# A deeper attention pipeline with a shorter second score pass, in a streaming encoder kernel

## The reference, cut to what matters

```python
def band_attend(q, kb, vb, bias, key_valid):
    s = jnp.einsum('bnthd,bnmhd->bnhtm', q, kb).astype(jnp.float32) * (HEAD_DIM ** -0.5)
    s = s + bias.astype(jnp.float32)[None, None]
    s = jnp.where(key_valid[None, :, None, None, :], s, NEG_INF)
    p = jax.nn.softmax(s, axis=-1).astype(vb.dtype)
    return jnp.einsum('bnhtm,bnmhd->bnthd', p, vb)
```

## Time and profile before

| | |
|---|---|
| Time, median of 3 runs | 2631.17 us (2630.45 to 2631.81) |
| Time of the profiled execution | 2631.02 us |
| Its span in the profile | 2629.2 us, so 1.8 us lie around it |
| PE busy | 2567.8 us, 98% of the span |
| DVE, ACT, POOL busy | 1771.9, 1356.9, 556.9 us |
| Attention stage, from its first score product to the first merge product | 775.1 to 1013.15 us, 238 us |

### The profile page before, as it was taken

One profiled execution on the slowest core, in us unless ns is written; L12 is line 12 of the kernel. 1 busy time (PEld: TensorE's weight loads), 2 busy tenths in 40 slices (PEclk: granted clock), 3 DMA queues, 4 the chain that ended last, 5 costly groups with the idle time before them and its releaser, 6 DMA issues.

```text
span 2629.2 us, 49866 instructions
## 1 busy us (share of the span) xinstructions
PE 2567.8 (98%) x18164; PEld 1678.0 (64%) x18164; DVE 1771.9 (67%) x3413; ACT 1356.9 (52%) x2632; POOL 556.9 (21%) x645
## 2 busy tenths in 40 slices
PE   6999899999999999999999999999999999999998
PEld 2466566666666665559986666666666666666665
DVE  5967577587746665566787798888888874242433
ACT  4967374564747773124566555555555553121211
POOL 2600000000017772000001354434333321101000
PEclk8999999999999999999999999999999999999999
DMA  8622513233365432555542445554555449566662
GB/s 294 201 87 88 197 52 137 93 124 133 104 181 122 114 121 107 181 191 148 146 117 86 142 171 176 185 182 157 174 185 180 138 136 349 196 246 233 236 247 95
DMA packets 243890, 424.07 MB, mean 161 GB/s; under 512 B 58424, under 2 KB 163384, under 8 KB 235528
## 3 DMA queue, kind: packets, MB, share of 16 engines
q1 hardware_dynamic: 234872, 413.08, 47.6%
q10 hardware_dynamic: 8848, 8.74, 1.0%
HBM read 284.47 MB, written 139.92 MB: 161 GB/s over the span
## 4 chain that ended last, share of the span: by engine, by line
PE 83%; DVE 5%; ACT 4%; DMA 3%; issue 2%; POOL 2%; SPq 1%; DVEq 0%; ACTq 0%; POOLq 0%
PE ps L3064 55%; PE ps L3319 14%; PE ps L3173 7%; PE ps L3163 2%; PE ps L3145 2%; PE ps L3132 1%; PE ps L3105 1%; POOL arena L1194 1%; ACT arena L1653 1%; DMA arena<-in_w_down 1%; DVE arena L2734 1%; ACT arena L1363 1%; DMA arena<-in_w_mod 1%; ACT arena L1329 1%; DMA arena<-in_w_mod_rest 1%
## 5 line engine op out<-in xcount | busy, mean ns | idle before, releaser
L3064 PE MATMUL ps<-arena 128*128 128x352 f16 (+1 forms) x11880 | 1612.8, 297 | 4.1 <-ACT arena L1821 1.9
L3064 PEld LDWEIGHTS ps<-arena 128*128 128x128 f16 x11880 | 1100.6, 97 | 511.8 <-ACT arena L1821 2.6
L3319 PE MATMUL ps<-arena 128*128 128x352 f16 x2772 | 415.0, 310 | 1.5 <-DVE arena L2763 1.2
L3319 PEld LDWEIGHTS ps<-arena 128*128 128x128 f16 x2772 | 264.7, 96 | 151.8 <-DVE arena L2763 1.5
L1226 POOL TENSOR_TENSOR arena<-arena 128x640 f32<-128x640 f32 (+5 forms) x136 | 150.2, 1123 | 707.5 <-DVE arena L2514 706.1
L1245 POOL TENSOR_TENSOR arena<-arena 128x128 f32<-128x128 f32 x44 | 30.9, 703 | 747.2 <-DMA arena<-in_w_down 746.9
L3173 PE MATMUL ps<-arena 128*128 128x424 f16 (+1 forms) x960 | 171.5, 341 | 0.0
L1813 ACT ACTIVATE arena<-ps 128x352 f32<-128x352 f32 x264 | 116.0, 460 | 94.7 <-PE ps L3064 94.7
L2866 DVE TENSOR_TENSOR arena<-ps,arena 128x352 f32<-128x352 f32 x12 | 6.3, 525 | 204.5 <-PE ps L3319 174.6
L3173 PEld LDWEIGHTS ps<-arena 128*128 128x128 f16 x960 | 92.5, 96 | 78.6
L1446 ACT ACTIVATE arena<-ps 128x352 f32<-128x352 f32 x192 | 80.4, 460 | 118.9 <-PE ps L3064 118.9
(11 more groups left out here) (239 smaller groups left out, 3293.4 us busy)
## 6 DMA issues: line engine op xcount, KB each, us to landing
hidden_combinations<-arena SPq DMA_DIRECT2D x48, 616.0 KB, 3.2
arena<-hidden_combinations SPq DMA_DIRECT2D x24, 1232.0 KB, 7.5
arena<-in_w_up SPq DMA_DIRECT2D x44, 512.0 KB, 5.0
down_combinations<-arena SPq DMA_DIRECT2D x44, 448.0 KB, 2.8
ffn_hidden<-arena SPq DMA_DIRECT2D x44, 440.0 KB, 3.1
arena<-down_combinations SPq DMA_DIRECT2D x10, 1792.0 KB, 7.6
arena<-down_combinations SPq DMA_DIRECT2D x20, 896.0 KB, 6.3
arena<-ffn_hidden SPq DMA_DIRECT2D x50, 352.0 KB, 4.0
```

What stands on the lines that cost most here:

```text
L3064: mm = pe.matmul(out, wt[:, k, wp, :], act_t[:, k, hp], start=(first and k == 0 and n == 0), stop=(last and k == K - 1 and n == 2), skip_g ...
L3319: mm = pe.matmul(ps[:, down_bank(n, k), 0:CF].rearrange("p (w t) -> p w t", w=2), dwt(i)[:, wi, wp, :], dact[i][:, :, bi, hp, :], start=(i ...
```

## The change

It has four parts.

1. Order on PE: scores of tile c, then the transposes of tile c - 2, then the value products, which come one cycle later than before (`Group.end` is one more). DVE and ACT get new orders to match, and one cycle more at the end. `inverse_sums` of head 1 moves into the next cycle.
2. Three probability buffers in place of two; the waits that guard them are loosened (`t_filled` by two units).
3. The second score pass contracts only the high half of the queries (64 rows) with the low part of the keys. Head 0 lies on partitions 0 to 63 and head 1 on 64 to 127. The order of the score products is new too: the first pass of both heads, then the short second pass of both heads in alternation. `s_filled` of both heads is raised at the end.
4. The low keys are stored once, not twice: per head group two loads fewer (10 in place of 12 on `at_loaded`), half the bytes of low keys, and two steps of `cached_halves` fewer (6 in place of 8).

```diff
-        pr = [at_(o, 2 * BAND).rearrange("p (h n) -> p h n", h=2) for o in (45120, 13056)]
+        pr = [at_(o, 2 * BAND).rearrange("p (h n) -> p h n", h=2) for o in (45120, 13056, 14336)]
...
-                self.end = self.last.tile + (3 if self.m < LOTS - 2 else 2)
+                self.end = self.last.tile + (4 if self.m < LOTS - 2 else 3)
... (ACT)
-            for c in range(NTILE + 2):
-                if c < NTILE:
-                    exps(Unit(2 * c))
-                for G in ended_in(c):
+            for c in range(NTILE + 4):
+                for G in ended_in(c - 1):
                     out_hi(G)
-                if c < NTILE:
-                    exps(Unit(2 * c + 1))
-                if 0 < c <= NTILE:
-                    for h in range(2):
-                        probs(Unit(2 * c - 2 + h))
+                for h in range(2):
+                    if 2 <= c < NTILE + 2:
+                        probs(Unit(2 * c - 4 + h))
+                    if c < NTILE:
+                        exps(Unit(2 * c + h))
... (DVE)
-            for c in range(NTILE + 2):
+            for c in range(NTILE + 4):
                 if c < NTILE:
                     scores(Unit(2 * c))
-                    scores(Unit(2 * c + 1))
-                    inverse_sums(Unit(2 * c))
                 if 0 < c <= NTILE:
-                    probs(Unit(2 * c - 2))
-                for G in ended_in(c):
+                    inverse_sums(Unit(2 * c - 1))
+                for G in ended_in(c - 1):
                     out_lo(G)
                 if c < NTILE:
-                    inverse_sums(Unit(2 * c + 1))
-                if 0 < c <= NTILE:
-                    probs(Unit(2 * c - 1))
+                    scores(Unit(2 * c + 1))
+                if 2 <= c < NTILE + 2:
+                    probs(Unit(2 * c - 4))
+                    probs(Unit(2 * c - 3))
+                if c < NTILE:
+                    inverse_sums(Unit(2 * c))
... (PE)
+                pieces = [(bank, c, x.k0 + 512 * bank) for bank, c in ((0, min(x.w, 512)), (1, x.w - 512)) if c > 0]
+                q = slice(x.q0, x.q0 + x.rows)
+                for y in units:
+                    keep_above_zero(pe, s_added, y.u - 1)
+                    for bank, c, k in pieces:
+                        pe.matmul(ps[0:x.rows, 2 * y.h + bank, 0:c], qs[x.b][:, y.h, q], khh[x.b][:, y.h, k:k + c],
+                                  start=True, stop=False)
+                for bank, c, k in pieces:
+                    for y in units:
+                        hi = slice(64 * y.h, 64 * y.h + 64)
+                        mm = pe.matmul(ps[0:x.rows, 2 * y.h + bank, 0:c], qs[x.b][hi, y.h, q], kll[x.b][hi, k:k + c],
+                                       start=False, stop=True)
...
-            for c in range(NTILE + 2):
+            for c in range(NTILE + 3):
                 if c < NTILE:
-                    scores(Unit(2 * c))
-                    scores(Unit(2 * c + 1))
+                    scores(Unit(2 * c), Unit(2 * c + 1))
+                if 2 <= c < NTILE + 2:
+                    probs(Unit(2 * c - 4))
+                    probs(Unit(2 * c - 3))
                 for G in parts_in(c):
                     outs(G, c)
-                if 0 < c <= NTILE:
-                    probs(Unit(2 * c - 2))
-                    probs(Unit(2 * c - 1))
```

More of the change, by code:

```diff
@@ L159, in build @@
         khh = [v.rearrange("p (h t) -> p h t", h=2) for v in of_set(2112, 2 * KEYS, F16)]
-        kll = [v.rearrange("p (h t) -> p h t", h=2) for v in of_set(4736, 2 * KEYS, F16)]
+        kll = of_set(4736, KEYS, F16)
         vv = [v.rearrange("p (i d) -> p i d", d=P) for v in of_set(7360, 21 * P)]
@@ L394, in build @@
         w_loaded = [sem(f"w_loaded{i}") for i in range(3)]
-        y_loaded, Y_BASE = (at_loaded[0], at_loaded[1], bias_loaded, kc_loaded), (384, 384, 16 * NJ, 16 * NJ)
+        y_loaded, Y_BASE = (at_loaded[0], at_loaded[1], bias_loaded, kc_loaded), (320, 320, 16 * NJ, 16 * NJ)
         q_filled = sem("q_filled")
@@ L834, in _ @@
                                  bass.AP(bias_d.tensor, P - 1, [[768, 8], [-1, P], [1, BAND]])).then_inc(band_stored, 16)
+            KEY_PIECES = ((0, TP, 0), (TP, T, TP + PAST))
             def queries_and_keys(j):
@@ L841, in queries_and_keys @@
                         sp.dma_start(qs[b][half, h, :], q_d[j, 64 * h:64 * h + 64, (h + g) % 2]).then_inc(s, 16)
[L842 to L845, removed]
+                    for t0, t1, k0 in KEY_PIECES:
+                        sp.dma_start(khh[b][half, :, k0:k0 + t1 - t0],
+                                     k_d[j, :, 0, t0:t1].rearrange("(h p) t -> p h t", p=64)).then_inc(s, 16)
+                for t0, t1, k0 in KEY_PIECES:
+                    sp.dma_start(kll[b][:, k0:k0 + t1 - t0], k_d[j, :, 1, t0:t1]).then_inc(s, 16)
             def values_and_bias(j):
@@ L856, in cached_keys @@
                 if j:
-                    sp.wait_ge(kc_hi, 8 * j)
+                    sp.wait_ge(kc_hi, 6 * j)
                 sp.dma_start(craw, a["cache_kT"][j]).then_inc(kc_loaded, 16)
@@ L1202, in cached_halves @@
                 pool.wait_ge(kc_loaded, 16 * j + 16)
-                keep_above_zero(pool, kc_hi, 8 * j)
+                keep_above_zero(pool, kc_hi, 6 * j)
                 if j >= 2:
@@ L1210, in cached_halves @@
                 for h in range(2):
-                    pool.wait_ge(kc_hi, 8 * j + 2)
+                    pool.wait_ge(kc_hi, 6 * j + 2)
                     pool.tensor_copy(khh[b][own[1 - h], h, cols], khh[b][own[h], h, cols]).then_inc(kc_hi, 1)
                     yield
-                    pool.tensor_tensor(kll[b][own[h], h, cols], craw[own[h]], khh[b][own[h], h, cols], ALU.subtract)\
+                    pool.tensor_tensor(kll[b][own[h], cols], craw[own[h]], khh[b][own[h], h, cols], ALU.subtract)\
                         .then_inc(kc_hi, 1)
                     yield
-                for h in range(2):
-                    pool.wait_ge(kc_hi, 8 * j + 4 + 2 * h)
-                    pool.tensor_copy(kll[b][own[1 - h], h, cols], kll[b][own[h], h, cols]).then_inc(kc_hi, 1)
-                    yield
             def scaled(x):
-                own = pr[x.tile % 2][0:x.rows, x.h, 0:x.w]
+                own = pr[x.tile % 3][0:x.rows, x.h, 0:x.w]
                 pool.wait_ge(r_ready, x.u + 1)
@@ L1232, in _ @@
                 for h in range(2):
-                    keep_above_zero(pool, kc_hi, 8 * j + min(8, max(0, i - 4)))
+                    keep_above_zero(pool, kc_hi, 6 * j + min(6, max(0, i - 4)))
                     scaled(Unit(2 * c + h))
-                if 4 <= i < 12:
+                if 4 <= i < 10:
                     pool.wait_ge(p_scaled, 2 * c + 2)
@@ L1652, in exps @@
                 keep_above_zero(act, r_ready, x.u - 3)
-                act.activation(pr[b][0:x.rows, x.h, 0:x.w], pr[b][0:x.rows, x.h, 0:x.w], ACT.Exp, scale=-1.0,
+                own = pr[x.tile % 3][0:x.rows, x.h, 0:x.w]
+                act.activation(own, own, ACT.Exp, scale=-1.0,
                                bias=least[0:x.rows, x.h:x.h + 1],
@@ L2491, in scores @@
                 dve.wait_ge(s_filled, x.u + 1)
-                keep_above_zero(dve, t_filled, x.u - 3)
+                keep_above_zero(dve, t_filled, x.u - 5)
                 if w > 512:
@@ L2497, in scores @@
                 dve.memset(mark[:, h:h + 1], 0.0)
-                dve.tensor_tensor_reduce(pr[x.tile % 2][0:rows, h, 0:w], src, bias[x.b][0:rows, h, x.b0:x.b0 + w], 1.0, 3.0e38,
+                dve.tensor_tensor_reduce(pr[x.tile % 3][0:rows, h, 0:w], src, bias[x.b][0:rows, h, x.b0:x.b0 + w], 1.0, 3.0e38,
                                          ALU.add, ALU.min, least[0:rows, h:h + 1]).then_inc(s_added, 1)
@@ L3119, in _, with scores @@
             pe.wait_ge(p_ev, 6 * NR)
-            def scores(x):
+            def scores(*units):
+                x = units[0]
                 if x.i == 0:
-                    pe.wait_ge(at_loaded[x.b], 192 * (x.j // 2) + 192)
+                    pe.wait_ge(at_loaded[x.b], 160 * (x.j // 2) + 160)
                 if x.sample:
[L3125 to L3134, removed]
+                    pe.wait_ge(kc_hi, 6 * x.j + 6)
+                pieces = [(bank, c, x.k0 + 512 * bank) for bank, c in ((0, min(x.w, 512)), (1, x.w - 512)) if c > 0]
[10 more added lines that the diff above has]
+                                       start=False, stop=True)
+                        if bank == pieces[-1][0]:
+                            mm.then_inc(s_filled, 1)
             def probs(x):
@@ L3145, in probs @@
                     mm = pe.transpose(ps[0:k, bank, c0:c0 + x.rows],
-                                      pr[x.tile % 2][0:x.rows, x.h, c * P:c * P + k], ident[0:x.rows, 0:x.rows])
+                                      pr[x.tile % 3][0:x.rows, x.h, c * P:c * P + k], ident[0:x.rows, 0:x.rows])
                 mm.then_inc(t_filled, 1)
```

1 line of the change is left out of this document (removed).

## The result

| | before | changed |
|---|---|---|
| median | 2631.49 us (2630.45 to 2632.91, 4 runs) | 2672.64 us (2670.64 to 2674.5, 4 runs) |
| span of the profiled execution | 2629.2 us | 2671.4 us |
| ratio, 95% interval | 1 | 1.0157 (1.0143 to 1.0171) |

The account below looks back on a forecast made before the run. PE, busy 98% of the span, was taken to bound the kernel. A new loop through DVE in wide cycles (+50 us) less narrow-tile gains (-8) gave +42 on 2631.02: 2673 us, range 2650 to 2697.

Parts of the forecast that it names:

- The loop: Wide cycles: scores, DVE passes, copy, last transpose, value products in series; 4.87 us against 3.74, +50 us over 44 cycles.
- the DVE term: DVE's part of each wide cycle: score pass 0.82, reciprocal 0.16, score pass 0.82, copy 0.29, together 2.09 us.
- the low end: Wide cycles if score passes overlap (-0.14) and out_lo hides (-0.17): 2655 us, widened to 2650.
- a wait over 1 us in 44 cycles: Expected in the profile after: PE's last transpose waits on the fifth-block copy, 50 to 65 us in all.
- 4.7 to 5.0: Expected in the profile after: length in us of a wide cycle, from scores to scores.
- What is given back: Narrow tiles: PE's waits for POOL and ACT mostly vanish, 2 us per head group, -8 us; bounds 0 and -12.
- a pipeline one cycle deeper should take most of that: Narrow tiles: the deeper pipeline removes most of PE's 2.2 us idle in 16.36, giving 2 us per group.
- The end of the stage: One more cycle at the end of the attention stage adds no work; 0 us.
- The short passes ran side by side: Score products on PE: two heads' short passes run together, 0.27 us; the rival, one after another, 2685 us, 15%.
- The clock: Rival, 5%: PE's clock falls half the time in the wide cycles, +41 us, 2714 us.
- It does what its words say: Rival, 7%: in wide cycles the last transpose never waits and PE is the bound at 3.55 us; 2615 us.
- The two rules: On PE: products keep program order, so value products stand behind the wait; each tiling-mode switch drains the array, costing 0.09 us.

Follow-up runs that it names:

- e1: The changed kernel with DVE's copy of head 0's fifth block moved directly behind the first score pass; 2632.91 us, ratio 1.001.
- e2: The changed kernel with the fifth blocks of both heads transposed together, after the first four blocks of both; 2625.27 us, ratio 0.9981.
- e7: The changed kernel with one unread DVE fill added directly before the copy of head 0's fifth block; 2689.38 us, ratio 1.0228.
- e4: The changed kernel with full 128-row second score passes per head and low keys stored twice, as before; 2649.65 us, ratio 1.0079.
- e5: The kernel of e2 with out_lo moved ahead of the first score pass on DVE; 2621.11 us, ratio 0.9964.
- e6: The kernel of e5 with the full 128-row second score pass per head, low keys stored twice; 2618.27 us, ratio 0.9953.

## Why the prediction was right

The sign and the cause are as forecast. That the size came out within 1 us is luck: three terms were off, and their errors cancel. From tile to tile on PE's timeline the 42 us lie so:

| part of the stage | forecast | measured |
|---|---|---|
| wide cycles (scores of tile 6 to the next group's tile 0) | +50, 44 cycles | +31.5 in the first three groups, +7.9 in the last up to its last tile's scores: +39.4, 43 cycles |
| narrow tiles (scores of tile 0 to tile 6) | -8 | -1.9 in the first group, +0.3 in each of the others: -0.9 |
| from the scores of the last tile to the merge | 0 | +3.7 |
| sum | +42 | +42.2 |

**The loop, +50 forecast.** The place, the releaser and the order of steps are as forecast; e1 takes the wait away by moving the copy, e2 by another order on PE, e7 lengthens it one to one. The size: on the timeline of PE the scores of tile 6 of the second group start at 858.14 and those of the next group's tile 0 at 909.32, 51.2 us for the 11 cycles, against 848.61 to 889.30, 40.7, before. That is +0.95 us a cycle, not +1.13. In the last group it is less, since there the kernel before had one long wait of 1.25 us of its own on the same copy. Step by step for the cycle at 885.90: handed over to DVE after 1.14 (forecast 1.12); first pass 0.75, reciprocal 0.08, second pass 0.75, copy 0.29, together 1.87 (forecast 2.09); `out_lo` 0.32 every second cycle (0.33); to PE 0.05 (0.05); last transpose to value products 0.26 (0.20); value products 1.24 (1.24). The error is the DVE term, mis-sized by 0.22 us: each instruction lets the next in before it is done. I had named 0.14 of that, of the two score passes, in the low end; the other 0.08 is the reciprocal. So the forecast's sign of a wait over 1 us in 44 cycles holds for every other cycle only (1.15 and 0.82 us in turn, 46.7 us in all where 50 to 65 were named), and the wide cycles are 4.88 and 4.55 us where 4.7 to 5.0 were.

**What is given back, -8 forecast.** It was nothing in the narrow tiles of all groups but the first. From the scores of tile 0 to those of tile 6 it took 17.7 us before (830.91 to 848.61) and takes 18.0 (840.10 to 858.14). e4 shows why. There these six cycles take 16.4 us (832.16 to 848.58): the deeper pipeline does give back 1.3 us a group. The short pass and the new order of the scores that comes with it take 1.6 us again. Both heads are handed to DVE only when both are done, and the first pass of head 1 must wait until DVE has read its bank. The timeline of the changed kernel has it for tile 4, which is scored while the narrow tile 2 is transposed; the first line is the first pass of head 1:

```profile
852.97 0.45 PE L3131 MATMUL ps<-arena 128*128 128x512 f16 x2 [0.37 <-DVE arena L2496]
853.35 0.45 PE L3136 MATMUL ps<-arena 64*128 64x512 f16 x4
```

The step that failed is thus not "a pipeline one cycle deeper should take most of that", which e4 bears out, but what the sum left out: what the late handing over costs where PE's work is short. It was put at nothing, and with the rest of parts 3 and 4 it measured 1.6 us a group. In the wide cycles it is part of the loop: the changed kernel takes 51.2 us for them, e4 47.4. The second group as a whole lost 10.8 us (840.10 to 909.32 against 830.91 to 889.30).

**The end of the stage, 0 forecast.** From the first score product of the last tile to the first merge product it was 1013.08 - 1003.84 = 9.2 us before and is 1055.88 - 1042.96 = 12.9 us: the pipeline has one more cycle to empty, and with nothing else in flight that cycle is not hidden. Its last wait, 1.03 us of the value products for `out_lo`, is new; before, they waited 0.47 us for ACT there.

**The rivals.** The short passes ran side by side: four products took 0.38 us with their switch (886.55 to 886.93), and one after the other they would have needed 0.55 alone. The clock stayed at 1.00 from the second group on. "It does what its words say" needed the copy done 2.4 us after the scores' start; it was done at 3.3 (889.23 - 885.90).

**The two rules.** The order of products was kept: the twelve value products start 0.26 us after the late transpose, in the changed kernel (889.28 to 889.54) as in e4 (872.94 to 873.20). The Trainium skill, TensorE: Matmul & The Clock Gate, Part 3, says that products start and end strictly in program order, and by that rule the trace agrees. Switches cost what the earlier trace rows had said, or a little more: the first pass of both heads takes 0.65 us to the short pass for 0.55 of products, and the short pass 0.38 for 0.27. The 0.27 us of products that the short pass saves shrink to 0.07 on the way to the transposes (e5 against e6), about what these two switches leave of them (0.27 - 0.10 - 0.11). The Trainium skill, TensorEngine Tiling (Array Packing), Key Properties, says that a change of tiling mode drains the engine; the trace agrees in so far as each of the three changes measured here costs 0.09 to 0.11 us.

Not settled: why e5's longer cycles are 3.57 and not 3.51 us, and whether the 2.8 us between e5 and e6 are real, since their intervals overlap; their traces differ by 0.55 us over the whole second group (55.68 and 55.13), which would be some 2 us in four. How the 1.6 us a group divide between the late handing over and the rest of parts 3 and 4 was not taken apart either.

## What to carry to other kernels

A wait is only as short as what stands before its releaser on the other engine: before moving an instruction on one engine, look where the instruction that releases it stands in the other engine's list, and what that list waits for itself. When an engine is full, put its waiting instruction last in a block and its independent work ahead; here one DVE copy of 0.29 us in the wrong place cost 40 us, and two transposes at the end of the block were worth 6 us in the old kernel. Of a pass that is halved by array tiling, count the two switches against the saving first, and look at whether its result is handed over later: in the changed kernel that cost more than the pass could save.

## What was not expected of the hardware

A DVE reciprocal of one column, 0.16 us by itself, let the next instruction start 0.08 us after it, and a score pass of 0.82 us let it start after 0.75. In a loop it is the distance between starts that counts; the durations overstated the loop by 0.2 us a cycle. Products of 64 rows on the two halves of the array do run side by side: four of them, 512 and 128 wide for two heads, took 0.38 us with a switch, where four products as wide on the whole array take 0.55.
